# First mixer's front: another order on ScalarE, VectorE, TensorE and in the loads

## The reference, cut to what matters

```python
mod = (silu(c) @ w_mod[l] + b_mod[l])            # shift, scale, gate: six rows of 1024
h = x * (1.0 + sc1) + sh1
proj = h @ w_in[l]                               # 2776 columns
aq, ak, av, iq, ik, iw, bq, bk, bv, bg, ba = split(proj)
# sparse attention: an indexer scores the keys, the best 64 of each query are kept
s_idx  = relu(einsum('bthd,bsd->bths', iq, ik) * idx_scale)
scores = einsum('bth,bths->bts', iw, s_idx)
sel    = top_k(where(causal, scores, -inf), 64)
y_a    = softmax_attention(aq, ak[sel], av[sel], alibi)
# gated linear attention with a decay from a rank-16 projection
log_a = log_sigmoid(ba @ w_a2 + b_a) / 16
b     = cumsum(log_a)
attn  = einsum('bthd,bshd,bhtsd->bhts', bq, bk, exp(b_t - b_s))   # t >= s
o     = rms_norm(attn @ bv) * gla_g * silu(bg)
y     = concat([y_a, o]) @ w_out[l]
x     = layer_norm(ALPHA * x + (1.0 + g1) * y)
```

## Time and profile before

| | us |
|---|---|
| median of 3 runs | 1236.26 (1230.97 to 1237.36) |
| profiled execution, its time | 1236.48 |
| profiled execution, its span | 1234.6 |

### The profile page before, as it was taken

One profiled execution on the slowest core, in us unless ns is written; L12 is line 12 of the kernel. 1 busy time (PEld: TensorE's weight loads), 2 busy tenths in 40 slices (PEclk: granted clock), 3 DMA queues, 4 the chain that ended last, 5 costly groups with the idle time before them and its releaser, 6 DMA issues.

```text
span 1234.6 us, 25919 instructions
## 1 busy us (share of the span) xinstructions
PE 1149.0 (93%) x11052; PEld 656.3 (53%) x11052; DVE 540.1 (44%) x884; ACT 283.6 (23%) x486; POOL 67.3 (5%) x118
## 2 busy tenths in 40 slices
PE   1889899999999898699999999999999999999995
PEld 1789777778878798423333324334334344343342
DVE  6799867777768999740121111021111201201226
ACT  0556343333426563310010010010100100100100
POOL 3100010000112000010000000000000000000011
PEclk9999999999999999899999999999999999999998
DMA  9974778999956747999999999999999999999991
GB/s 344 311 254 137 270 259 315 350 371 397 335 180 195 264 137 248 409 385 369 411 399 410 411 397 400 412 399 414 411 385 412 413 397 411 408 399 412 411 403 64
DMA packets 156955, 423.12 MB, mean 343 GB/s; under 512 B 21053, under 2 KB 75105, under 8 KB 145569
## 3 DMA queue, kind: packets, MB, share of 16 engines
q1 hardware_dynamic: 146720, 395.16, 83.9%
q0 software_dynamic: 6080, 20.31, 4.5%
q10 hardware_dynamic: 4032, 5.90, 1.4%
HBM read 405.60 MB, written 15.73 MB: 341 GB/s over the span
## 4 chain that ended last, share of the span: by engine, by line
PE 69%; DVE 5%; issue 2%; DMA 2%; ACT 1%; POOL 0%; SPq 0%; DVEq 0%; ACTq 0%
PE bank L1399 37%; PE bank L1413 18%; PE bank L347 4%; PE bank L349 3%; PE bank L348 3%; DVE mod_acc L1563 1%; DMA u_raw<-in_w_in_dram 1%; DVE u_low L1574 1%; DMA raw_u<-in_ffn_w_up_dram 1%; PE bank L982 1%; PE bank L1128 0%; PE bank L1388 0%; DVE ycat L1586 0%; DVE stats L1588 0%; DVE ycat L1585 0%
## 5 line engine op out<-in xcount | busy, mean ns | idle before, releaser
L1399 PE MATMUL bank<-raw_w,xg 128*32 128x512 f32 (+1 forms) x4608 | 468.0, 560 | 9.8 <-issue 7.2
L1399 PEld LDWEIGHTS bank<-raw_w,xg 128*32 128x32 f32 x4608 | 180.5, 110 | 289.4 <-issue 251.3
L1947 DVE TENSOR_TENSOR he<-he,bank 128x256 f32<-128x256 f32 (+1 forms) x72 | 25.6, 383 | 529.4 <-ACT he L913 529.4
L1413 PE MATMUL bank<-raw_w,heT 128*32 128x512 f32 x2112 | 237.5, 592 | 0.0
L1413 PEld LDWEIGHTS bank<-raw_w,heT 128*32 128x32 f32 x2112 | 79.9, 110 | 146.9 <-issue 145.1
L913 ACT ACTIVATE he<-bank 128x256 f32<-128x256 f32 (+1 forms) x72 | 21.2, 367 | 582.7 <-PE bank L1399 582.7
L1563 DVE SCALAR_TENSOR_TENSOR mod_acc<-mod_row,c_act,mod_acc 128x1024 f32<-128x1024 f32 x63 | 80.8, 1283 | 5.1
L347 PE MATMUL bank<-u_high,hT_H 128*128 128x256 f32 x256 | 75.1, 294 | 2.0 <-DVE u_low L1574 1.1
L349 PE MATMUL bank<-u_high,hT_L 128*128 128x256 f32 x256 | 72.2, 282 | 0.0
L348 PE MATMUL bank<-u_low,hT_H 128*128 128x256 f32 x256 | 72.1, 282 | 0.0
L347 PE MATMUL bank<-gu_H,hT_H 128*128 128x512 f32 x160 | 64.8, 405 | 0.0
(11 more groups left out here) (302 smaller groups left out, 1255.9 us busy)
## 6 DMA issues: line engine op xcount, KB each, us to landing
raw_w<-in_moe_w_down_dram SPq DMA_DIRECT2D x88, 1024.0 KB, 13.0
raw_w<-in_moe_w_gate_dram SPq DMA_DIRECT2D x128, 512.0 KB, 11.3
raw_w<-in_moe_w_up_dram SPq DMA_DIRECT2D x128, 512.0 KB, 13.6
mod_row<-in_w_mod_dram SPq DMA_DIRECT2D x80, 512.0 KB, 6.9
raw_w<-in_moe_w_gate_dram SPq DMA_DIRECT2D x64, 384.0 KB, 9.8
raw_w<-in_moe_w_up_dram SPq DMA_DIRECT2D x64, 384.0 KB, 12.3
u_raw<-in_w_in_dram SPq DMA_DIRECT2D x20, 1024.0 KB, 8.0
raw_d<-in_ffn_w_down_dram SPq DMA_DIRECT2D x11, 1024.0 KB, 11.0
```

Source lines behind the costliest of these rows:

```text
L1399: last = mm(bank[g][32 * q:32 * q + 32, 0:2 * HALF[c]].rearrange("s (m j r) -> s m j r", m=2, r=64), xg[:, i, g, k, :], cols[:, :, :, 64 * ...
L1413: last = mm(bank[3 + g][32 * q:32 * q + 32, :], heT[(par + c) % 2][:, g, 2 * a + b, :], W[:, b, h * 512:(h + 1) * 512], start=(c == 0 and ...
L1947: V.tensor_tensor(h, h, bank[g][:, w:2 * w].rearrange("s (j c b) -> s j b c", b=2, c=32), ALU.mult).then_inc(s["m_hid"], 1)
```

## The change

For the first layer alone:

- ScalarE makes the tokens' high part ahead of the high part of U_BK, and copies U_BQ and U_BA out ahead of the high part of U_IQ0.
- TensorE multiplies U_BK ahead of the decay's small products, where it did so behind them.
- VectorE: the rows 0 and 1 of w_mod are taken behind the low part of U_IQ1 and no longer ahead of it; rows 2 and 3 behind `decay_keys` and no longer ahead of `decay`; the low part of U_KEYS comes ahead of `decay_keys`.
- SP loads rows 0 and 1 behind U_IQ1 (they were behind U_IQ0), rows 2 and 3 behind U_AQ0 (behind U_IQ1), rows 4 and 5 behind U_AQ1 (behind U_KEYS).

No instruction is added or taken away.

```diff
-            rows_after_unit = ({3: (0, 1), 4: (2, 3), 5: (4, 5), 8: (6, 7), 9: (8, 9, 10, 11), 15: (12, 13)},
+            rows_after_unit = ({4: (0, 1), 6: (2, 3), 7: (4, 5), 8: (6, 7), 9: (8, 9, 10, 11), 15: (12, 13)},
@@ ScalarE, mixer(l)
-                conv_unit(l, U_BK)
                 if l:
+                    conv_unit(l, U_BK)
                     normalise(2 * l - 1)
-                high_of_tokens(2 * l)
-                conv_unit(l, U_IQ0)
-                evacuate(l, U_BQ)
-                evacuate(l, U_BA)
+                    high_of_tokens(2 * l)
+                    conv_unit(l, U_IQ0)
+                    evacuate(l, U_BQ)
+                    evacuate(l, U_BA)
+                else:
+                    high_of_tokens(0)
+                    conv_unit(0, U_BK)
+                    evacuate(0, U_BQ)
+                    evacuate(0, U_BA)
+                    conv_unit(0, U_IQ0)
                 conv_unit(l, U_IQ1)
                 decay_in(l)
@@ TensorE, mixer(l)
                 project(l, U_BA)
+                if l == 0:
+                    project(l, U_BK)
                 pe.wait_ge(s["evac"], l * NIN + U_BA + 1)
...
-                for u in (U_BK, U_IQ0, U_IQ1, U_KEYS):
+                for u in (U_IQ0, U_IQ1, U_KEYS) if l == 0 else (U_BK, U_IQ0, U_IQ1, U_KEYS):
                     project(l, u)
@@ VectorE, mixer(l)
                 low_unit(l, U_IQ0)
                 if l:
                     norm_out(1)
-                else:
-                    condition_rows(range(0, 2))
                 low_unit(l, U_IQ1)
                 if l == 0:
+                    condition_rows(range(0, 2))
+                decay(l)
+                if l:
+                    decay_keys(l)
+                    low_unit(l, U_KEYS)
+                else:
+                    low_unit(l, U_KEYS)
+                    decay_keys(l)
                     condition_rows(range(2, 4))
-                decay(l)
-                decay_keys(l)
-                low_unit(l, U_KEYS)
                 decay_products(l)
```

## The result

| | us |
|---|---|
| before, median of 20 runs | 1234.36 (1230.97 to 1238.22) |
| changed, median of 20 runs | 1238.45 (1235.87 to 1241.48) |
| ratio, with its 95% interval | 1.0028 (1.0020 to 1.0036) |
| the same in a second job | 1.0025 (1.0014 to 1.0036) |
| changed, profiled execution: span | 1235.6 |

The change makes the kernel slower by 0.28%, which is 3.5 us (2.5 to 4.4); the two medians differ by 4.1. The forecast was +1.6 us on the profiled time, 1238.1. The single profiled span is only 1.0 us longer than before, so one span alone would have told little; the stages inside it tell more.

A forecast was written before the change was run, and what follows sets the result against it. The prediction took VectorE's list up to the indexer, then one relu, then TensorE as the bound. It added +0.1 (indexer) and +1.5 (clock) to the profiled 1236.5 us, giving 1238.1, with an 8-in-10 range of 1232.0 to 1241.0.

The forecast's parts named there:

- its two terms: First mixer: +0.1 us for the indexer's later start and +1.5 us for TensorE's slower clock behind it.
- Nothing is gained on VectorE: Before the indexer: VectorE's freed 4.9 us go as idle pieces before U_BK's, U_IQ0's and the next low part, and the decay.
- The loads cost nothing: First mixer: the reordered loads cost nothing; U_IQ1 lands at 46.8 us, within bounds of 46.4 to 49.0.
- The late-load rival: U_IQ1's load lands at 49.0 as before, indexer at 79.1, +3.4 us with the clock's 1.5, total 1239.9; chance 0.18.
- From the decay to the indexer 23.28 us: VectorE's work from the decay's start at 53.95 to the indexer, rows 2 and 3 included, takes 23.28 us.
- +0.1 for the indexer: VectorE starts the indexer at 77.2 us, where it did before; taken as +0.1, bounds −0.5 and +1.9.
- my sign of being wrong: Wrong if the indexer starts before 76 or after 78 us, or if TensorE restarts at clock 1.00.
- +1.5 for the clock: TensorE's wait before the third relu grows to 6.5 us; half rate for 3.0 us at U_AQ0 then loses 1.5 us.
- My upper bound: Clock loss at U_AQ0 of at most 3.0 us, from a half-clock stretch twice as long.
- The sum: Whole kernel: +0.1 + 1.5 = +1.6 us on the profiled 1236.5, so 1238.1; chance 0.47.
- The rival with no fall of the clock: TensorE's clock doesn't fall behind the gap before the third relu; total 1236.6 us; chance 0.20.
- The one with a real gain: VectorE idles only for U_BK, so the indexer starts at 71.7, 5.5 us sooner; total 1231.0; chance 0.07.

The follow-up runs named there:

- rows and loads: The kernel before with only VectorE's and SP's parts of the change; ratio to before 1.0020.
- TensorE kept busy: The changed kernel plus 11 spare products in TensorE's list ahead of the wait for the third relu; ratio to before 1.0043.
- the control: The changed kernel plus 11 spare products at the start, where TensorE waits for the first loads; ratio to before 1.0053.
- small products first: The changed kernel with TensorE's part undone, the decay's small products ahead of U_BK again; ratio to before 1.0023.
- half ahead: The kernel before, reordered to start the decay early, with half of U_AQ0's products ahead of the third relu's wait; ratios to before 0.9988 and 0.9994.
- whole U_AQ0 ahead: The changed kernel with all 48 products of U_AQ0 moved ahead of the wait for the third relu; ratio to before 1.0029.

## Why the prediction was right, and by how much it was off

- *The number.* 1238.1 was forecast and the median is 1238.45, but that they are so near is luck. The forecast was added to a profiled execution of 1236.5, and this lies 2.1 us above before's median over 20 runs, 1234.4. The change itself was forecast at +1.6 and measured at +3.5 (2.5 to 4.4), so its two terms together are less than half of what was measured.
- *Nothing is gained on VectorE.* Right. The 4.9 us in one piece came back as 0.58, 4.15, 1.57 and 1.04 us, 7.3 in all, against 7.2 forecast in the same four places. One by one they were forecast as 1.6, 3, 1.3 and 1.3: U_BK's copy began 1 us sooner than I counted, and the next piece grew by as much.
- *The loads cost nothing.* Right in the stages: U_IQ1's copy starts 15.1 us from the first slice in the first profile (forecast 14.9) and 16.0 in the second, where U_BQ, which releases the load, ended 0.9 us later; and no row of VectorE waits for a load. The late-load rival didn't occur. The total of rows and loads alone, 1.0020, leaves a doubt that the stages don't explain.
- *From the decay to the indexer 23.28 us.* Right: 23.2, with ScalarE's wait of 0.68 gone.
- *+0.1 for the indexer.* Too small. It is +0.4 and, in the second pair of profiles, +2.0; +1.2 as a mean. I had carried over U_BQ's and U_BA's ends (41.3 and 42.3) as if they were fixed. In the kernel before nothing hung on them, since the decay waited for U_IQ1's load. In the changed kernel the decay waits for TensorE's first three blocks, and what U_BQ takes longer reaches VectorE one for one: U_BQ ended 0.4 and 1.4 us later than the 9.4 from the first slice that I carried over, and the decay began 0.4 and 1.4 us later than forecast. With the small products ahead of U_BK the decay is at 22.2 and the indexer at 45.4. So my sign of being wrong, an indexer behind 78 "(a load was late)", came true in the second profile (78.5, counted as there) for another reason.
- *+1.5 for the clock.* Right in mechanism, too small. From L1174 or L1182 to U_AQ1's copy it is 12.6 us in both profiles of before (91.97 − 79.37 in the first) and 14.7 and 15.2 in those of the changed kernel: +2.1 and +2.6. I took the 3.0 us at 0.50 from the earlier trace rows as all that would fall on work. Behind 6.45 us of nothing the half clock lasts until 85.9 us, so about 4.7 us of it lie on work, and in the second profile until 87.0, 5.6 us; half of that is 2.3 and 2.8 us. My upper bound, twice the row's length, covered it. The Trainium skill ("TensorE: Matmul & The Clock Gate", HAM oscillation) says that an idle gap leaves the array throttled for the products that follow it; the trace agrees, with 0.50 behind 6.45 us.
- *The sum.* 1.2 + 2.35 = 3.55 us as the mean of two profiles each, and the ratio says 3.5 (2.5 to 4.4). The layer norm is 2.8 and 4.4 us later than before. With stages that vary by 0.7 to 0.9 us from one profile of a kernel to the other, the close agreement of the means is partly luck.
- *What the clock costs and what the order costs.* The 2.4 us behind the indexer are the clock's: with TensorE kept busy they vanish (73.2 from the indexer to the layer norm, 74.9 in the control), and with the gap moved the half clock moves along. The 1.2 us ahead of the indexer come from the order, which made the decay wait for TensorE; this size is less sure, as two profiles of one kernel differ there by 0.7 and 0.9 us. That the whole kernel would get its time back with TensorE kept busy isn't shown, since the spare products cost time behind the first mixer.

The rival with no fall of the clock is out: half clock in all four profiles with a gap over 6 us. The one with a real gain is out too, as the indexer is no sooner in either profile. A second fall of the clock, which I hadn't foreseen, shows in both profiles of the changed kernel at about 134 us (0.50 from 135 to 136), and not in the two of before. It cost little: small products first has it too and takes 75.7 us from the indexer to the layer norm, the control with the spares at the start hasn't and takes 74.9; half ahead has it and takes 73.2.

## What to carry to other kernels

A wait that goes is worth nothing until the list behind it is read for the next thing that isn't there: here the engine that sets the pace idled for the same time in four pieces instead of one. Making an engine early that has slack can cost time, because its slack gathers in one gap, and behind that it runs at half clock on the path. And a wait that stops depending on a load and starts depending on another engine inherits that engine's variations; in the sum their mean is to be put in, not the one value of the profiled execution.

## What the runs showed of the hardware

- The length of an idle gap of TensorE doesn't settle by itself whether half clock follows. Gaps of 6.15 to 6.46 us were followed by it each time (four profiles), and so were 4.14 and 3.81 us (the two profiles of before), 3.10 us at 46 (rows and loads) and 3.44 us (whole U_AQ0 ahead). 3.0 us before U_BV0 was once and once not, and 2.7 and 1.8 us were not; but 1.75 us was in whole U_AQ0 ahead. The gap of 2.0 us at about 130, the same in all thirteen profiles, was followed by half clock in five.
- Half clock behind a gap of over 6 us cost 2.1 and 2.6 us, for 4.7 and 5.6 us of work at 0.50.
- Twenty-two TensorE instructions (11 products) added at a place where the engine idles anyway cost 4.3 us in the median. The gap at each jump back of a loop far behind them was 2.4 and 2.6 us at the first jump and 2.0 and 2.3 at the second in the two profiles without them, and 3.5 and 3.6 us with them.
